# One indirect transfer for u and v rows, a ring of four groups of two, and dot products one group ahead

## The chip, the cores and the metric

The kernel runs on one core of a Trainium2 chip. The metric is the device time of one execution in microseconds (us). The core has TensorE (matrix products into PSUM), VectorE (DVE), ScalarE (ACT), GpSimd (POOL) and SyncE (SP), each with its own instruction queue, and 16 DMA engines between HBM and the on-chip SBUF. Engines meet only at semaphores.

## The reference

Two layers of a decoder trunk on 256 tokens of width 1024, all in float32. Each layer has a mixer (attention, pooling, a gated recurrence) and then a retrieval layer over 16384 single-neuron experts, which the change touches:

```
q = (xt @ w_query).reshape(T, 8, 2, 128)
s = einsum('thpd,pkd->thpk', q, sub_keys)
s_a, i_a = top_k(s[:, :, 0], 16);  s_b, i_b = top_k(s[:, :, 1], 16)
top_s, idx = top 16 of the 256 sums s_a + s_b   # expert = i_a * 128 + i_b
gate = softmax(top_s)
act = gelu(einsum('thkd,td->thk', u_tab[idx], x))
out = einsum('thk,thkd->td', gate * act, v_tab[idx])
```

For every token and each of 8 heads 16 experts are chosen; each brings a row of 1024 numbers of u and one of v. That is 256 x 8 x 16 x 2 rows of 4 KB per layer, 268 MB.

## The kernel before

The program is written by hand, with semaphores between engines. Per layer there is a mixer (a loop over pairs of its 8 heads) and then the expert stage. The expert stage is a loop over 8 heads. A head has 8 groups: 4 groups for the tokens 0 to 127 (`t` = 0) and 4 for the tokens 128 to 255 (`t` = 1); a group is 4 of the 16 chosen experts of each of the 128 tokens, one token to a partition. `gi` numbers the groups of a head from 0 to 7 and `q` those of a half from 0 to 3.

The order on each engine:

- GpSimd: `gather_u(gi + 1)` (L536), then `gather_v(gi)` (L546). Each issues four indirect transfers; one transfer brings one row of 4 KB to each of 128 partitions, 0.52 MB. u goes to `ubuf`, a ring of two groups of four rows in `wbuf[0]`; v to `vbuf`, the same in `wbuf[1]`. `gather_u` waits until the dot products two groups before are done, `gather_v` until the sum two groups before is done.
- VectorE: `dot_group(gi)` (recorded at L967, four reductions of 1024 elements, each with a small read of the accumulator), then a part of the routing for the next half, then `diag_group(gi)` (recorded at L961): four diagonal matrices of 128x128, with gate times gelu on the diagonal. The routing is `route_half` at `q` = 0 and 1 (top 16 of 128 scores, from L1284 on) and `route_pairs` with `route_end` at `q` = 2 (top 16 of the 256 sums, from the cast at L958 on, up to indices and gates).
- ScalarE: the gelu of each group (L681). At `gi` = 2 it then does the softmax exponentials of the routing (L675) and `q_evac(h + 1)`, the copy of the next head's queries from PSUM (L671). It does this before the gelu of group 3.
- TensorE: `expert_sum(gi)` (L922): for each of the four experts two matmuls of the diagonal with half a row of v, added up in PSUM, sixteen matmuls in all. After the sum of group 2 it makes the queries of the next head (`queries`, L900, 32 matmuls) and ahead of the sum of group 3 its key scores (`key_scores`, L910).
- SyncE loads the query weights of the next heads, 1 MB each, when the queries before them are done (L332). At the start of the second layer it loads the mixer's weights over `wbuf` (L349): the first part of `wbuf[0]` when the last dot products are done, that of `wbuf[1]` when the last sum is done.

After the last head VectorE adds the sums to the residual (`add_experts`, L1376 and L1378).

Of the kernel before, what the change touches and what calls it, by code (L numbers as in the profile page):

```python
# [25 lines left out]
P = 128  # L26
D = 1024
# [16 lines left out]
GROUP = 4  # L44
# [26 lines left out]
PEER_CHAIN = 99  # L71
# [9 lines left out]


def dotted(l):

    return (LGROUPS + 1) * l + 1
# [22 lines left out]
def build(nc, x, c, ada_w, ada_b, norm_mix_g, w_in, diff_lambda, diff_subln_g, pool_w, pool_scale,  # L108
          hgrn_lower_bounds, hgrn_norm_g, w_out, norm_ffn_g, peer_w_query, peer_sub_keys,
          peer_u, peer_v, final_g, out):  # L110
    with ExitStack() as ctx:
        def sb(name, shape, dt=F32):
            return ctx.enter_context(nc.sbuf_tensor(name, shape, dt))
# [21 lines left out]
        ubuf = wbuf[0][:, 0:2 * GROUP * D].rearrange("p (b s d) -> p b s d", b=2, s=GROUP)  # L135
        vbuf = wbuf[1][:, 0:2 * GROUP * D].rearrange("p (b s d) -> p b s d", b=2, s=GROUP)
# [25 lines left out]
        diag = M[:, 1024:2048].rearrange("p (b s n) -> p b s n", b=2, s=GROUP)  # L162
# [65 lines left out]
        dots = [sb(f"dots{b}", [P, GROUP]) for b in range(2)]  # L228
        gel = [sb(f"gel{b}", [P, GROUP]) for b in range(2)]
# [10 lines left out]
        s_u = [sem("s_u0"), sem("s_u1")]  # L240
        s_v = [sem("s_v0"), sem("s_v1")]
# [40 lines left out]
        u_rows = peer_u.rearrange("l e d -> (l e) d")  # L282
        v_rows = peer_v.rearrange("l e d -> (l e) d")


        WTAIL = range(-(-2 * GROUP * D // (SECT * P)), KC)
# [22 lines left out]
        def _(sp):  # L309
# [36 lines left out]
            for l in range(DEPTH):  # L346
# [22 lines left out]
                if l == 0:  # L369
                    load_w(0, 0)  # L370
                    sp.wait_ge(s_chunk, ADA_CHUNKS)
                    load_w(1, 1)
                else:

                    load_w(0, 0, WTAIL)
                    load_w(1, 1, WTAIL)
                    sp.wait_ge(s_dot, dotted(l - 1) + LGROUPS)
                    load_w(0, 0, range(WTAIL[0]))
                    sp.wait_ge(s_vacc, summed(l - 1) + LGROUPS)
                    load_w(1, 1, range(WTAIL[0]))  # L380
                    sp.wait_ge(s_peer, l)
                    load_bias_row(l, 2 * D, 6 * D)
# [39 lines left out]
        def _(pool):  # L422
# [49 lines left out]
            for l in range(DEPTH):  # L472
# [54 lines left out]
                def gather_u(h, gi):  # L527
                    t, q = gi // GROUPS, gi % GROUPS
                    if q == 0:
                        pool.wait_ge(s_route, h * NT + (2 * HEADS * l + t + 1))  # L530
                    if l or gi or not isinstance(h, int) or h:
                        pool.wait_ge(s_dot, h * HGROUPS + (dotted(l) + gi - 1))
                    apart(pool)
                    for s in range(GROUP):
                        k = q * GROUP + s
                        nc.gpsimd.indirect_dma_start(  # L536
                            out=ubuf[:, gi % 2, s, :], out_offset=None, in_=u_rows,
                            in_offset=bass.IndirectOffsetOnAxis(ap=idx[t][:, k:k + 1], axis=0)).then_inc(s_u[gi % 2], 16)

                def gather_v(h, gi):  # L540
                    t, q = gi // GROUPS, gi % GROUPS
                    pool.wait_ge(s_vacc, h * HGROUPS + (summed(l) + gi - 1))
                    apart(pool)
                    for s in range(GROUP):
                        k = q * GROUP + s
                        nc.gpsimd.indirect_dma_start(  # L546
                            out=vbuf[:, gi % 2, s, :], out_offset=None, in_=v_rows,
                            in_offset=bass.IndirectOffsetOnAxis(ap=idx[t][:, k:k + 1], axis=0)).then_inc(s_v[gi % 2], 16)

                def head(h, more):  # L550
                    for gi in range(HGROUPS):
                        if gi + 1 < HGROUPS:
                            gather_u(h, gi + 1)
                        elif more:
                            gather_u(h + 1, 0)
                        gather_v(h, gi)

                gather_u(0, 0)
                with pool.Fori(0, HEADS - 1) as h:
                    head(h, True)  # L560
                head(HEADS - 1, False)
# [4 lines left out]
        def _(act):  # L566
# [11 lines left out]
            for l in range(DEPTH):  # L578
# [110 lines left out]
                route_exp(0, 0)  # L689
                with act.Fori(0, HEADS - 1) as h:  # L690
                    head(h, True)
# [4 lines left out]
        def _(pe):  # L696
# [26 lines left out]
            for l in range(DEPTH):  # L723
# [171 lines left out]
                def queries(h):  # L895

                    pe.wait_ge(s_r[0], h * 16 + 16 * (ADA_CHUNKS // 4 + (HEADS - 1) * l))
                    for a in range(2):
                        for k in range(KC):
                            i = mm(bank(B_Q)[:, a * T:(a + 1) * T], ringv[0][:, k, a * P:(a + 1) * P], hT[:, k, :],  # L900
                                   start=(k == 0), stop=(k == KC - 1))
                    i.then_inc(s_chunk, 1)
# [11 lines left out]
                def expert_sum(h, gi, last=False):  # L914

                    t = gi // GROUPS
                    pe.wait_ge(s_diag, h * HGROUPS + (LGROUPS * l + gi + 1))
                    pe.wait_ge(s_v[gi % 2], h * (16 * HGROUPS * GROUP // 2)
                               + 64 * (LGROUPS // 2 * l + gi // 2 + 1))
                    for s in range(GROUP):  # L920
                        for hf in range(2):
                            i = mm(bank(B_ACC + 2 * t + hf), diag[:, gi % 2, s, :],  # L922
                                   vbuf[:, gi % 2, s, hf * 512:(hf + 1) * 512], start=False,
                                   stop=(last and s == GROUP - 1), skip_group_check=True)
# [12 lines left out]
                for b in range(4):  # L937
                    i = mm(bank(B_ACC + b), diag[:, 1, GROUP - 1, :], hT[:, 0:2, :], start=True, stop=False,
                           skip_group_check=True)
                    i.then_inc(s_vacc, 1)  # L940
# [12 lines left out]
        def _(dve):  # L953
# [118 lines left out]
            for l in range(DEPTH):  # L1072
# [205 lines left out]
                v.memset(dots[1][:], 0.0).then_inc(s_dot, 1)  # L1278
                v.memset(diag[:, 1, GROUP - 1, :], 0.0).then_inc(s_cb, 1)
# [68 lines left out]
                def dot_group(h, gi):  # L1348
                    t = gi // GROUPS
                    dve.wait_ge(s_u[gi % 2], h * (16 * HGROUPS * GROUP // 2) + 64 * (LGROUPS // 2 * l + gi // 2 + 1))  # L1350

                    for s in range(GROUP):
                        u = ubuf[:, gi % 2, s, :]
                        i = dot(u, u, tok[:, t, :], dots[gi % 2][:, s:s + 1])
                        if s < GROUP - 1:
                            ch(i)
                    i.then_inc(s_dot, 1)

                def diag_group(h, gi):
                    t, q = gi // GROUPS, gi % GROUPS  # L1360
                    dve.wait_ge(s_gel, h * HGROUPS + (LGROUPS * l + gi + 1))
                    dve.wait_ge(s_vacc, h * HGROUPS + (summed(l) + gi - 1))
                    for s in range(GROUP):
                        k = q * GROUP + s
                        i = sts(diag[:, gi % 2, s, :], ident[:], gel[gi % 2][:, s:s + 1], gate[t][:, k:k + 1],
                                ALU.mult, ALU.mult)
                        if s < GROUP - 1:
                            ch(i)
                    i.then_inc(s_diag, 1)
# [10 lines left out]
                def head(h, more):  # L1380
                    for gi in range(HGROUPS):
                        if gi == HGROUPS - 2 and not more:
# [3 lines left out]
                        dot_group(h, gi)  # L1386
# [11 lines left out]
                        ch.sync()  # L1398
# [5 lines left out]
                route_end(0, 0, True)  # L1404
                start = ch.n
# [20 lines left out]
        "peer_u", "peer_v", "final_g"]  # L1426
# [16 lines left out]
```

## Time and profile before

| | |
|---|---|
| time, median of 3 runs | 2810.35 us (2802.63 to 2813.17) |
| span of the profiled execution | 2765.2 us; its own time is not given apart, so the median of the runs stands beside it |
| expert stage, core 0 | about 604 to 1410 us and 1950 to 2750 us |
| busy over the span | PE 76%, DVE 69%, POOL 57%, ACT 12% |
| DMA | 715 MB, of which 536.94 MB in the indirect gathers; mean 259 GB/s |
| indirect gathers | 1024, half of them u and half v |

The span is the time from the first to the last instruction of the core in the execution that the profiler recorded; what the metric counts beyond it lies before and after. Times in the profile are counted from the start of the span. An engine's line in the profile carries the line number of the code that recorded it, its operation, what it wrote and what it read. "Idle before" is how long the engine stood before that instruction, and the arrow names what ended the standing.

### The profile page before, as it was taken

The numbers are of one execution on the slowest core, as the hardware profiler recorded it, in microseconds if no ns is written. First come the engines' busy times: TensorE is split into PE (matmuls) and PEld (weight loads), VectorE is DVE, ScalarE is ACT, GpSimd is POOL, SyncE is SP. The second block draws the span as 40 slices with busy tenths as digits, with TensorE's granted clock in tenths as the row PEclk, the third lists the DMA queues.
The fourth block names the chain that finished last, engine by engine and source line by source line (L and its number), as shares of the span: only waits on it lengthen the run. The fifth ranks groups of instructions, "written<-read, shape, count | busy, mean of one in ns | idle before, by whom it ended". The sixth has DMA issues, their size and how long they took to land.

```text
span 2765.2 us, 23903 instructions
## 1 busy us (share of the span) xinstructions
PE 2103.5 (76%) x6485; PEld 1236.6 (45%) x6485; DVE 1907.0 (69%) x4313; ACT 333.0 (12%) x696; POOL 1582.3 (57%) x1421
## 2 busy tenths in 40 slices
PE   6988887757777777867779889896577767767766
PEld 5766665533333323323247657664233323323322
DVE  3588888956666576675635888888566576576664
ACT  0211112100011011010002221120011011011010
POOL 1445554436766776776731433332667776676775
PEclk9989898778898989988889988997799998989988
DMA  9645555239999999998973565421799999999996
GB/s 310 172 130 142 137 151 164 77 134 329 364 340 359 365 342 347 361 381 322 359 227 104 146 169 147 114 98 63 269 341 359 371 329 335 357 346 340 335 357 252
DMA packets 405255, 715.06 MB, mean 259 GB/s; under 512 B 20667, under 2 KB 270803, under 8 KB 405075
## 3 DMA queue, kind: packets, MB, share of 16 engines
q0 software_dynamic: 147456, 536.94, 52.6%
q1 hardware_dynamic: 257750, 177.54, 22.6%
q8 instruction: 22, 0.36, 0.1%
q14 instruction: 27, 0.22, 0.0%
HBM read 713.35 MB, written 1.05 MB: 258 GB/s over the span
## 4 chain that ended last, share of the span: by engine, by line
PE 29%; POOL 22%; DVE 21%; issue 17%; DMA 8%; ACT 2%; SPq 1%; DVEq 0%; POOLq 0%; ACTq 0%
POOL wbuf L536 12%; PE PS L922 10%; POOL wbuf L546 9%; DMA wbuf<-in_peer_v,idx 7%; PE PS L749 5%; PE PS L900 4%; PE PS L812 3%; PE PS L744 3%; DVE M L1101 3%; DVE wbuf L967 2%; DVE ring L964 2%; DVE ring L1173 2%; DVE ring L1172 1%; DVE tok L964 1%; ACT ring L632 1%
## 5 line engine op out<-in xcount | busy, mean ns | idle before, releaser
L922 PE MATMUL PS<-wbuf,M 128*128 128x512 f32 x2048 | 1040.7, 667 | 451.5 <-DMA wbuf<-in_peer_v,idx 421.6
L922 PEld LDWEIGHTS PS<-wbuf,M 128*128 128x128 f32 x2048 | 427.1, 214 | 1054.8 <-issue 845.0
L536 POOL DMA_INDIRECT wbuf<-in_peer_u,idx x512 | 652.8, 1275 | 301.9 <-issue 152.0
L967 DVE CUSTOM_DVE_ANT_0 wbuf<-wbuf,tok 128x1024 f32<-128x1024 f32 x512 | 597.6, 1222 | 256.9 <-DMA wbuf<-in_peer_u,idx 256.6
L546 POOL DMA_INDIRECT wbuf<-in_peer_v,idx x512 | 498.7, 974 | 160.5 <-issue 154.6
L961 DVE TENSOR_SCALAR M<-ident,gel,gate 128x128 f32<-128x128 f32 x512 | 144.0, 355 | 266.9 <-ACT gel L681 248.5
L744 PE MATMUL PS<-hT,wbuf 128*128 128x256 f32 x1280 | 285.1, 382 | 6.0 <-DMA wbuf<-in_w_in 5.2
L467 POOL TENSOR_SCALAR rsb<-ms 128x4 f32<-128x4 f32 (+2 forms) x23 | 4.4, 193 | 481.3 <-DVE ms L967 481.3
L744 PEld LDWEIGHTS PS<-hT,wbuf 128*128 128x128 f32 x1280 | 243.6, 191 | 41.3 <-issue 6.7
L749 PE MATMUL PS<-wbuf,hT 128*128 128x512 f32 x512 | 231.3, 606 | 0.0
L485 POOL TENSOR_TENSOR braw<-braw,cact 128x1024 f32<-128x1024 f32 x80 | 154.2, 1928 | 65.8 <-DMA braw<-in_ada_w 65.8
L812 PE MATMUL PS<-ring 128*128 128x64 f32 x448 | 93.3, 401 | 128.2 <-DVE ring L1195 128.2
L812 PEld LDWEIGHTS PS<-ring 128*128 128x128 f32 x448 | 90.8, 313 | 140.8 <-DVE ring L1195 139.8
L681 ACT ACTIVATE gel<-dots 128x4 f32<-128x4 f32 x128 | 26.3, 205 | 1049.3 <-DVE dots L967 1049.1
L749 PEld LDWEIGHTS PS<-wbuf,hT 128*128 128x128 f32 x512 | 99.8, 198 | 112.9 <-issue 112.1
L754 PE MATMUL PS<-wbuf,hT 128*128 128x256 f32 x512 | 113.1, 379 | 0.0
L487 POOL TENSOR_TENSOR braw<-braw 128x512 f32<-128x512 f32 x80 | 107.9, 1349 | 6.3
L1118 DVE RECIPROCAL M<-M 128x1024 f32<-128x1024 f32 x16 | 104.8, 6553 | 0.6
L754 PEld LDWEIGHTS PS<-wbuf,hT 128*128 128x128 f32 x512 | 96.7, 190 | 13.7 <-issue 1.0
L900 PE MATMUL PS<-hT,ring 128*128 128x256 f32 x448 | 99.0, 379 | 0.0
L900 PEld LDWEIGHTS PS<-hT,ring 128*128 128x128 f32 x448 | 85.1, 190 | 17.5 <-issue 6.7
L1101 DVE RECIPROCAL M<-M 128x768 f32<-128x768 f32 x16 | 79.2, 4953 | 0.6
(223 smaller groups left out, 2130.4 us busy)
## 6 DMA issues: line engine op xcount, KB each, us to landing
wbuf<-in_w_in SPq DMA_DIRECT2D x128, 704.0 KB, 8.6
braw<-in_ada_w SPq DMA_DIRECT2D x80, 512.0 KB, 3.7
ring<-in_peer_w_query SPq DMA_DIRECT2D x16, 1024.0 KB, 8.5
wbuf<-in_w_out SPq DMA_DIRECT2D x2, 4096.0 KB, 16.0
wbuf<-in_peer_u,idx POOLq DMA_INDIRECT x512, 6.1
wbuf<-in_peer_v,idx POOLq DMA_INDIRECT x512, 6.2
ring<-in_ada_w SPq DMA_DIRECT2D x4, 1024.0 KB, 9.2
wbuf<-in_ada_w SPq DMA_DIRECT2D x4, 1024.0 KB, 12.0
```

The costliest lines, as they stand in the source:

```text
L485: pc(tt(w, w, cact[:, 4 * s:4 * s + 4].unsqueeze(2).to_broadcast([P, 4, CH]), ALU.mult))
L536: nc.gpsimd.indirect_dma_start(out=ubuf[:, gi % 2, s, :], out_offset=None, in_=u_rows, in_offset=bass.IndirectOffsetOnAxis(ap=idx[t][:, k: ...
L546: nc.gpsimd.indirect_dma_start(out=vbuf[:, gi % 2, s, :], out_offset=None, in_=v_rows, in_offset=bass.IndirectOffsetOnAxis(ap=idx[t][:, k: ...
L744: ins = mm(b[:, i * T:(i + 1) * T], wz[j][:, k, s, :], hT[:, k, :], start=(k == 0), stop=(k == KC - 1))
L749: ins = mm(b, hT[:, k, t * P:(t + 1) * P], wz[j][:, k, HI:ZP + 1, :], start=(k == 0), stop=(k == KC - 1))
L754: ins = mm(b[:, t * 256:(t + 1) * 256], hT[:, k, t * P:(t + 1) * P], wz[j][:, k, AV:ZR + 1:ZR - AV, :], start=(k == 0), stop=(k == KC - 1))
L812: mm(bank(b)[:, o + 64 * ck:o + 64 * ck + 64], XD[:, lv, ck * P:(ck + 1) * P], right, start=True, stop=True)
L900: i = mm(bank(B_Q)[:, a * T:(a + 1) * T], ringv[0][:, k, a * P:(a + 1) * P], hT[:, k, :], start=(k == 0), stop=(k == KC - 1))
L922: i = mm(bank(B_ACC + 2 * t + hf), diag[:, gi % 2, s, :], vbuf[:, gi % 2, s, hf * 512:(hf + 1) * 512], start=False, stop=(last and s == GR ...
L961: return v.tensor_scalar(o, a, s1, s2, op0, op1)
L967: return v.tensor_tensor_reduce(out=o, in0=a, in1=b, scale=1.0, scalar=0.0, op0=ALU.mult, op1=ALU.add, accum_out=acc)
L1101: ch(v.reciprocal(e, e))
```

## The change

The u and v tables come to the kernel as one table `peer_uv`, in which the 1024 numbers of u and the 1024 of v of an expert lie side by side. One indirect transfer brings both, 8 KB to each of 128 partitions. A group is now 2 experts instead of 4, so a head has 16 groups, 8 for each half. The ring has four slots, two in each `wbuf`, each of two experts with u and v; they take the same space as before. A slot is gathered again when the sum of the group in it is done.

VectorE does the dot products of group `gi + 1` ahead of the routing part and the diagonals of group `gi`; ScalarE does the gelu likewise one group ahead. The routing parts still stand at `q` = 0, 1 and 2. On TensorE the queries are split in two, after the sums of groups 2 and 3, and the key scores come after the sum of group 5. On ScalarE the copy of the queries stands at `gi` = 5, after the gelu of group 6.

```
-GROUP = 4
+GROUP = 2
+NBUF = 4
...
+        PAIRED = 2 * GROUP * 2 * D
+        uvbuf = [wbuf[b // 2][:, (b % 2) * (PAIRED // 2):(b % 2 + 1) * (PAIRED // 2)].rearrange("p (s d) -> p s d", s=GROUP)
+                 for b in range(NBUF)]
...
-                    sp.wait_ge(s_dot, dotted(l - 1) + LGROUPS)
+                    sp.wait_ge(s_vacc, summed(l - 1) + LGROUPS - 2)
                     load_w(0, 0, range(WTAIL[0]))
...
+                def gather(h, gi):
                     t, q = gi // GROUPS, gi % GROUPS
+                    b = gi % NBUF
                     if q == 0:
                         pool.wait_ge(s_route, h * NT + (2 * HEADS * l + t + 1))
-                    if l or gi or not isinstance(h, int) or h:
-                        pool.wait_ge(s_dot, h * HGROUPS + (dotted(l) + gi - 1))
+                    if gi >= NBUF or not isinstance(h, int) or h:
+                        pool.wait_ge(s_vacc, h * HGROUPS + (summed(l) + gi - NBUF + 1))
                     apart(pool)
                     for s in range(GROUP):
                         k = q * GROUP + s
                         nc.gpsimd.indirect_dma_start(
+                            out=uvbuf[b][:, s, :], out_offset=None, in_=uv_rows,
+                            in_offset=bass.IndirectOffsetOnAxis(ap=idx[t][:, k:k + 1], axis=0)).then_inc(s_uv[b], 16)
...
+                def gelu(h, gi):
+                    act.wait_ge(s_dot, h * HGROUPS + (LGROUPS * l + gi + 1))
+                    nc.scalar.activation(gel[gi % NBUF][:], dots[gi % NBUF][:], ACT.Gelu).then_inc(s_gel, 1)
+
                 def head(h, more):
                     for gi in range(HGROUPS):
-                        act.wait_ge(s_dot, h * HGROUPS + (dotted(l) + gi + 1))
-                        nc.scalar.activation(gel[gi % 2][:], dots[gi % 2][:], ACT.Gelu).then_inc(s_gel, 1)
+                        if gi + 1 < HGROUPS:
+                            gelu(h, gi + 1)
+                        elif more:
+                            gelu(h + 1, 0)
                         if gi == 2:
                             route_exp(h, 1)
-                            if more:
-                                q_evac(h + 1)
+                        if gi == 5 and more:
+                            q_evac(h + 1)
                         if gi == GROUPS + 2 and more:
                             route_exp(h + 1, 0)
...
                 def head(h, more):
                     for gi in range(HGROUPS):
-                        if more and gi == 3:
+                        expert_sum(h, gi, not more and gi % GROUPS == GROUPS - 1)
+                        if more and gi in (2, 3):
+                            queries(h + 1, gi - 2)
+                        if more and gi == 5:
                             key_scores(h + 1)
-                        expert_sum(h, gi, not more and gi % GROUPS == GROUPS - 1)
-                        if more and gi == 2:
-                            queries(h + 1)
...
-                        dot_group(h, gi)
+                        if gi + 1 < HGROUPS:
+                            dot_group(h, gi + 1)
+                        elif more:
+                            dot_group(h + 1, 0)
                         t, q = gi // GROUPS, gi % GROUPS
...
                             elif q == 2:
                                 route_pairs(nh, nt)
                                 route_end(nh, nt, False)
-                        ch.sync()
+                                ch.sync()
                         diag_group(h, gi)
```

## Rows read from the trace of the kernel before

**Rows 1.** The page's costliest groups: count, busy us and mean ns, idle before.

```profile
L922 PE MATMUL PS<-wbuf,M 128*128 128x512 f32 x2048 | 1040.7, 667 | 451.5 <-DMA wbuf<-in_peer_v,idx 421.6
...
L536 POOL DMA_INDIRECT wbuf<-in_peer_u,idx x512 | 652.8, 1275 | 301.9 <-issue 152.0
...
L546 POOL DMA_INDIRECT wbuf<-in_peer_v,idx x512 | 498.7, 974 | 160.5 <-issue 154.6
```

**Rows 2.** The waits of GpSimd: us in total, times, longest.

```profile
POOL wbuf L546 <- issue: 154.6, 507, 0.3
POOL wbuf L536 <- issue: 152.0, 472, 6.7
POOL wbuf L536 <- DVE dots L967: 104.6, 13, 10.2
```

**Rows 3.** The chain that ended last, queries of two heads: start us, us, what.

```profile
659.59 6.92 PE PS L900 x32
...
1253.22 6.92 PE PS L900 x32
```

**Rows 4.** The timeline around the queries of one head: start us, us, instruction, idle before.

```profile
765.93 0.60 ACT L671 ACTIVATE M<-PS 128x512 f32<-128x512 f32 x1 [24.53 <-PE PS L900]
...
767.84 0.21 ACT L681 ACTIVATE gel<-dots 128x4 f32<-128x4 f32 x1
...
768.24 1.11 DVE L961 TENSOR_SCALAR M<-ident,gel,gate 128x128 f32<-128x128 f32 x4 [18.12 <-ACT gel L681]
769.27 1.22 DVE L967 CUSTOM_DVE_ANT_0 wbuf<-wbuf,tok 128x1024 f32<-128x1024 f32 x1
...
773.86 0.08 DVE L967 DVE_READ_ACCUMULATOR2_ANT dots<- 128x1 f32 x1
...
774.71 0.94 POOL L536 DMA_INDIRECT wbuf<-in_peer_u,idx  x1 [8.77 <-DVE dots L967]
```

**Rows 5.** Stretches of 4 us; last three columns: PE clock, DMA share, GB/s.

```profile
652.00:656.00 4.00, 4.00 (x7) 1.55 (x6) 0.00 (x0) 0.00 (x0) 3.08 (x4) 0.59 0.94 338
...
660.00:664.00 4.00, 4.00 (x21) 3.51 (x20) 0.00 (x0) 0.00 (x0) 2.91 (x4) 1.00 1.03 422
664.00:668.00 4.00, 3.31 (x19) 2.68 (x18) 0.00 (x0) 1.45 (x2) 0.94 (x1) 1.00 1.03 412
...
672.00:676.00 4.00, 4.00 (x10) 1.73 (x10) 3.69 (x13) 0.21 (x1) 0.70 (x1) 1.00 0.16 52
```

**Rows 6.** Line L536, first and fourth gather of the stage, each with its landing.

```profile
L536 POOL DMA_INDIRECT wbuf<-in_peer_u,idx x1: 1222/1222/1222, 603.6 to 603.6; - x1
...
DMA to landing us min/median/max: 4.4/4.4/4.4
...
L536 POOL DMA_INDIRECT wbuf<-in_peer_u,idx x1: 937/937/937, 607.6 to 607.6; - x1
...
DMA to landing us min/median/max: 6.0/6.0/6.0
```

**Rows 7.** The timeline of VectorE: start of a routing half, of the pairs, and diagonals behind.

```profile
618.24 0.29 DVE L1284 MAX8 sv<-PS 128x8 f32<-128x128 f32 x1
...
620.35 1.12 DVE L961 TENSOR_SCALAR M<-ident,gel,gate 128x128 f32<-128x128 f32 x4 [0.23 <-DVE iu L1287]
...
636.67 0.18 DVE L958 CAST idf<-iu 128x32 f32<-128x32 uint32 x1
...
643.53 1.11 DVE L961 TENSOR_SCALAR M<-ident,gel,gate 128x128 f32<-128x128 f32 x4
```

**Rows 8.** The timeline of TensorE: sums of a group after short and long idleness.

```profile
637.25 7.11 PE L922 MATMUL PS<-wbuf,M 128*128 128x512 f32 x16 [1.85 <-DMA wbuf<-in_peer_v,idx]
...
649.68 9.90 PE L922 MATMUL PS<-wbuf,M 128*128 128x512 f32 x16 [5.33 <-DMA wbuf<-in_peer_v,idx]
...
792.03 8.69 PE L922 MATMUL PS<-wbuf,M 128*128 128x512 f32 x16 [7.77 <-DMA wbuf<-in_peer_v,idx]
```

**Rows 9.** The chain that ended last, the last sum of the first layer.

```profile
1401.66 8.82 PE PS L922 x16
```

More of the change, by code:

```diff
@@ L109, in build @@
           hgrn_lower_bounds, hgrn_norm_g, w_out, norm_ffn_g, peer_w_query, peer_sub_keys,
-          peer_u, peer_v, final_g, out):
+          peer_uv, final_g, out):
     with ExitStack() as ctx:
@@ L227, in build @@
         gate = [sb(f"gate{t}", [P, TOPK]) for t in range(2)]
-        dots = [sb(f"dots{b}", [P, GROUP]) for b in range(2)]
-        gel = [sb(f"gel{b}", [P, GROUP]) for b in range(2)]
+        dots = [sb(f"dots{b}", [P, GROUP]) for b in range(NBUF)]
+        gel = [sb(f"gel{b}", [P, GROUP]) for b in range(NBUF)]
         s_par, s_x, s_bias, s_gain = sem("s_par"), sem("s_x"), sem("s_bias"), sem("s_gain")
@@ L239, in build @@
         s_pused = sem("s_pused")
-        s_u = [sem("s_u0"), sem("s_u1")]
-        s_v = [sem("s_v0"), sem("s_v1")]
+        s_uv = [sem(f"s_uv{b}") for b in range(NBUF)]
         s_out = sem("s_out")
@@ L281, in build @@
         wq_v = [peer_w_query[l].rearrange("(k p) n -> p k n", p=P) for l in range(DEPTH)]
-        u_rows = peer_u.rearrange("l e d -> (l e) d")
-        v_rows = peer_v.rearrange("l e d -> (l e) d")
-        WTAIL = range(-(-2 * GROUP * D // (SECT * P)), KC)
+        uv_rows = peer_uv.rearrange("l e d -> (l e) d")
+        WTAIL = range(-(-PAIRED // (SECT * P)), KC)
         def brow(v, n):
@@ L536, in gather_u, with head @@
                         nc.gpsimd.indirect_dma_start(
[L537 to L550, printed above, removed]
-                    for gi in range(HGROUPS):
[L552 to L561, printed above, removed]
+                            out=uvbuf[b][:, s, :], out_offset=None, in_=uv_rows,
+                            in_offset=bass.IndirectOffsetOnAxis(ap=idx[t][:, k:k + 1], axis=0)).then_inc(s_uv[b], 16)
+                def head(h):
+                    for gi in range(HGROUPS):
+                        gather(h, gi)
+                head(0)
+                with pool.Fori(1, HEADS) as h:
+                    head(h)
             rsqrt(NR * DEPTH, NT, D)
@@ L689, in _ @@
                 route_exp(0, 0)
+                gelu(0, 0)
                 with act.Fori(0, HEADS - 1) as h:
@@ L893, in _, with queries @@
                         i.then_inc(s_psc0, 1)
[L895 to L902, printed above, removed]
+                def queries(h, a):
+                    if a == 0:
+                        pe.wait_ge(s_r[0], h * 16 + 16 * (ADA_CHUNKS // 4 + (HEADS - 1) * l))
+                    for k in range(KC):
+                        i = mm(bank(B_Q)[:, a * T:(a + 1) * T], ringv[0][:, k, a * P:(a + 1) * P], hT[:, k, :],
+                               start=(k == 0), stop=(k == KC - 1))
+                    if a == 1:
+                        i.then_inc(s_chunk, 1)
                 def key_scores(h):
@@ L917, in expert_sum @@
                     pe.wait_ge(s_diag, h * HGROUPS + (LGROUPS * l + gi + 1))
[L918 to L919 removed]
                     for s in range(GROUP):
                         for hf in range(2):
[L922 to L923 removed]
+                            i = mm(bank(B_ACC + 2 * t + hf), diag[:, gi % NBUF, s, :],
+                                   uvbuf[gi % NBUF][:, s, D + hf * 512:D + (hf + 1) * 512], start=False,
                                    stop=(last and s == GROUP - 1), skip_group_check=True)
@@ L1277, in _ @@
                 dve.wait_ge(s_tok, 3 * l + 3)
-                v.memset(dots[1][:], 0.0).then_inc(s_dot, 1)
-                v.memset(diag[:, 1, GROUP - 1, :], 0.0).then_inc(s_cb, 1)
+                v.memset(diag[:, NBUF - 1, GROUP - 1, :], 0.0).then_inc(s_cb, 1)
                 def top8(vals, ids, src):
@@ L1348, in dot_group @@
                 def dot_group(h, gi):
-                    t = gi // GROUPS
-                    dve.wait_ge(s_u[gi % 2], h * (16 * HGROUPS * GROUP // 2) + 64 * (LGROUPS // 2 * l + gi // 2 + 1))
+                    t, b = gi // GROUPS, gi % NBUF
+                    per = HGROUPS // NBUF * 16 * GROUP
+                    dve.wait_ge(s_uv[b], h * per + (per * HEADS * l + 16 * GROUP * (gi // NBUF + 1)))
                     for s in range(GROUP):
-                        u = ubuf[:, gi % 2, s, :]
-                        i = dot(u, u, tok[:, t, :], dots[gi % 2][:, s:s + 1])
+                        u = uvbuf[b][:, s, 0:D]
+                        i = dot(u, u, tok[:, t, :], dots[b][:, s:s + 1])
                         if s < GROUP - 1:
@@ L1381, in head @@
                     for gi in range(HGROUPS):
-                        if gi == HGROUPS - 2 and not more:
+                        if gi == HGROUPS - 4 and not more:
                             ch(add_experts(0))
@@ L1404, in _ @@
                 route_end(0, 0, True)
+                ch.sync()
+                dot_group(0, 0)
                 start = ch.n
```

20 lines of the change are left out of this document (8 added, 12 removed).

## The prediction

> **What bounds the kernel now.** I read the page's costliest groups first, to see that the expert stage (TensorE L922, GpSimd L536 and L546, VectorE L967) is where the time is [rows 1]; then the waits of GpSimd; then the chain of waits for the length of a head; then the timeline of one head. The stage runs from the first gather at 603.6 us to the end of the last sum at 1401.66 + 8.82 = 1410.5 us [rows 6, 9]: 806.9 us per layer, of which a head takes (1253.22 - 659.59) / 6 = 98.9 us [rows 3]. Two layers of it are 58% of the span.
>
> In this stage GpSimd does nothing but issue gathers. Over both layers it is busy 652.8 + 498.7 us, has 152.0 + 154.6 us of issue gaps of 0.3 us, and waits 104.6 us for dot products [rows 1, 2]: 1562.7 us of two stages of 806.9. So the issuing queue is the pace. A gather costs it (652.8 + 498.7 + 306.6) / 1024 = 1.42 us on average, eight per group of four pairs of rows, 11.4 us; that is 91 us of a head's 98.9. The transfers are just behind: 412 to 422 GB/s where GpSimd issues without a break, 52 GB/s where it stopped [rows 5]. A head's 32 pairs of 1.049 MB and its 1.05 MB of query weights are 34.6 MB, at 412 GB/s 84 us.
>
> The 104.6 us have one cause, which comes once per head. ScalarE stands 24.53 us in the copy of the query scores (L671), because TensorE makes the queries only after group 2's sum; the gelu of group 3 is queued behind it, VectorE stands 18.12 us before the diagonals of group 3, the dot products of group 4 come late, and GpSimd stands 8.77 us [rows 4].
>
> **What the change takes away.** (a) Half of the 1024 issues. If a row of 8 KB costs an issue what one of 4 KB does, GpSimd has 32 x 1.42 = 45 us of work in a head where it had 91: the present bound is gone. If it costs as for two rows, 1.88 us busy instead of 0.94, GpSimd still has room (32 x 2.2 = 70 us). (b) The copy of the queries stands behind the gelu of group 6, two groups after the last query matmul, so ScalarE's stall, and 104.6 us of GpSimd's waiting, go. Both together would leave the transfers as the bound.
>
> **What it adds: a longer loop through the ring.** Before, a u slot was free at its dot products and a v slot was asked for later than its u. Now one slot holds both until the sum. With four slots, the chain is: diagonals of group i, sum of i, slot free, gather of i+4, dot products of i+4, diagonals of i+3 (VectorE does them in that order). That is three groups per turn. Its terms, for groups of two:
> - diagonals 0.6 (four take 1.11 to 1.13, rows 4 and 7);
> - sum 3.7: sixteen matmuls take 7.11 warm [rows 8], eight half of that and the end of the pipeline;
> - slot free to issue 0.75: dot end 773.86 + 0.08 to issue 774.71 [rows 4];
> - landing of the pair of transfers, 2.1 MB, from the start of the first issue: not shown by this trace. The same bytes as four u transfers took 607.6 + 6.0 - 603.6 = 10.0 us [rows 6]. That is the upper end for equal work, as the new second issue comes at 1.24 us and not at 4.0. The lower end: the first 0.52 MB took 4.4 us, 3.15 beyond its 1.25 at 421 GB/s, and 2.1 MB at that rate are 5.0, so 8.1 us. I take 8.9, near the middle. A transfer path quicker with long rows could go below, at the very least to the 4.4 us of a quarter of the bytes; I carry 7 as a point between, near the upper of the two.
> - two dot products 2.3: four run from 769.27 to 773.94 [rows 4].
>
> Sum 16.25 us for three groups, 5.4 us per group, where the transfers alone would ask 5.0. A head of 16 groups would be 87 us were there nothing else. The loop has thus no slack, and whatever stands between a dot product and its diagonals, or before a sum, comes on top:
> - routing on VectorE, twice a head: a half 620.35 - 618.24 = 2.1 (two of them), the pairs 643.53 - 636.67 = 6.8 [rows 7]. Before they lay under 11.4 us of issuing per group; now they stand in a group of 5.4.
> - queries on TensorE after sums 2 and 3: 6.92 in all, 3.5 each [rows 3]; key scores, eight matmuls of half that width, after sum 5: under 8/32 of 6.92 = 1.7, taken as 1.3.
> - TensorE's clock: with 1.85 us of idleness before them sixteen matmuls take 7.11, with 5.33 they take 9.90, with 7.77 8.69 [rows 8]. After the 5.33 the granted clock was 0.59 over 652 to 656 us, so mostly the 1.2 GHz level, and 1.00 from 660 [rows 5]. A sum that starts on the low level costs 1.6 to 2.8 more, say 2.3; I call it cold.
>
> I walked through a head with these terms: dot products of i+1 at the later of their landing and VectorE's being free; then routing; then diagonals of i; sum at the later of that and TensorE's being free; landing of i+4 9.65 after the sum, and at least 5.0 after the landing before it (7.5 once, with the query weights). Diagonals start, with a warm TensorE, at 0, 5.0, 14.7 (pairs), 17.6, 21.2, 30.9, 38.1, 45.4, 52.5, 60.0, 69.6 (pairs), 72.5, 76.2, 85.9, 90.9, 95.9, and the next head's first at 104.3. One sees it at group 5: sum 2 ends at 19.0, its slot's next pair lands at 28.6, and so diagonals 5 start at 30.9, although VectorE could have been there at 24. The 6.8 us of the pairs are never won back, since group 5 waits for the slot of group 2. TensorE idles 4.6, 6.0, 6.0 and 5.1 us before sums 0, 2, 10 and 13; all four cold give 111.1 per head, two of them about 107.7. I take 107.7: 6.0 lies above the 5.33 that was cold, the others near it.
>
> **Sum.** Per layer: first diagonals 18.3 us after the first gather (8.9, 5.0 for the second group, 2.3, half a routing 2.1); seven heads of 107.7, 754; the last head, without second routing and queries but with 4 us of adding the first half's result, 90 us to the end of its last sum. Together 862 for 806.9, so +55; both layers +110. The span 2765.2 would be 2875; outside the span lie 2810.35 - 2765.2 = 45 us (taken from the median, since the profiled execution's own time is not given apart), which stay. 2810 + 110 = 2920; the four-cold walk gives 895 per layer and +177, and with a share of that I say 2925.
>
> Edits costed at nothing: the reload of the next layer's weights waits for the sum of group 13 instead of the last dot product. It lies under the last sums; if that cover is gone it costs at most one sum of 8.8 us [rows 9], once. Semaphores and the missing memset are single instructions. 64 more gelus per layer at 0.21 us [rows 4] go to ScalarE, busy for 12% of the span. The smaller groups at the start and end save a few us per layer and are in the walk.
>
> The Trainium skill ("DMA: Bandwidth & Descriptors", section "Anatomy of one DMA — SWDGE (gpsimd) path") gives a transfer 2.0 us fixed and bytes over 436 GB/s, which speaks for fewer, larger gathers. By that a 0.52 MB gather would be 3.2 us, where the row shows 4.4 from the start of the issue; a pair would be 6.8 us by it, plus the issue. No run here shows a gather of 8 KB rows.
>
> **The rivals.**
> 1. The ring keeps up and the transfers are the bound, the change doing all it could: 34.6 MB at 412 GB/s, 84 us a head, about 690 a layer, -234 in all: 2575. For it: 422 GB/s in rows 5 and GpSimd's bound gone. Against: the walks with landings of 7.95 and 7 (rival 2) give 101.4 and 99.2 per head, and on that slope 84 would need a landing under 1 us. The chance of 0.04 is for an error in the walk.
> 2. The pair lands quicker and TensorE stays warm. The walk with 8.1 (near it 7.95) gives 101.4 per head and 811 per layer, +8 in all; with 7, 99.2 and 793, -28: 2782. It decides from a landing of 7.7 us downward. For it: fewer issues and descriptors. Against: nothing in rows 6 lands 2.1 MB under 8.1. The 6.8 us worked out above from the Trainium skill's page would fall to this rival. Chance 0.13 of being faster by it, 0.06 of no change.
> 3. Issuing 8 KB rows costs double, 0.94 us more on each of the two issues. The landing becomes 10.8; the walk with 10 gives 924 per layer (four cold) and about 3 us per head and us more: +280, 3090. For it: unknown descriptors. Against: an issue may go by rows, of which there are still 128. Chance 0.1.
> 4. The change doesn't do what it says: ScalarE's stall comes back in another place, as the gelu of group 7 is behind the copy. The queries are then two groups old; 3.5 us of stall per head at most, +50 on the forecast: 2975. Chance 0.07.
> 5. The forecast, 2925, its own range 2840 to 3000: chance 0.6.
>
> Slower by over 0.5% (14 us, about what a measurement of this kernel can tell from no change): 0.6 + 0.1 + 0.07 = 0.77; faster 0.04 + 0.13 = 0.17; same 0.06. For 8 in 10 the range goes from 2800, which takes in the walk with 8 us, to 3010; the 2 in 10 outside are rivals 1, 3 and half of 2.
>
> **What would show it.** Right: GpSimd's waits in the stage for TensorE's sum (L922), several us per group, in place of its issue gaps and of the 104.6; the transfers below 350 GB/s with dips after groups 2 and 10; a head of 104 to 111 us; DVE waiting for the gather, most before group 5's or 13's. ScalarE's copy of the queries without a wait of 20 us. Wrong: landings of a pair under 7.5 us, a head under 98, or rates steady above 390 GB/s. Then the loop is shorter than I walked it and the forecast falls.

## The result, and the profile after

The changed kernel takes 3003.8 us (2997.1 to 3005.3 in 4 runs), the kernel before 2806.5 in the runs beside it: a ratio of 1.070, interval 1.068 to 1.073. Slower by 197 us; the forecast was slower, by 115, and the time lies just inside the upper end of the range, 3010.

The costliest groups of the page (count, busy us and mean ns, idle before), to be read beside [rows 1]:

```profile
L909 PE MATMUL PS<-wbuf,M 128*128 128x512 f32 x2048 | 1112.2, 700 | 636.6 <-DVE M L948 635.9
L954 DVE CUSTOM_DVE_ANT_0 wbuf<-wbuf,tok 128x1024 f32<-128x1024 f32 x512 | 607.4, 1223 | 767.4 <-DMA wbuf<-in_peer_uv,idx 767.4
...
L532 POOL DMA_INDIRECT wbuf<-in_peer_uv,idx x512 | 547.0, 1068 | 1294.4 <-PE PS L909 1108.5
```

GpSimd's 1024 issues of 1151.5 us together are now 512 of 547.0. The mean of one is 1068 ns, where u had 1275 and v 974 (the medians are 937, 940 and 938): a row of 8 KB costs the issue what one of 4 KB did. The 104.6 us behind ScalarE's copy [rows 2] are gone. In their place stand 1108.5 us of waiting for the sum. The issuing queue has been freed, and it now waits for a slot ten times as long as it waited for dot products before.

The transfers show what that is worth. The middle of the first stage, in the kernel before and then in the changed one, and three stretches of one head of the changed kernel (last columns: TensorE clock, DMA share, GB/s):

```profile
700.00:1300.00 600.00, 443.85 (x1016) 204.44 (x1015) 388.45 (x1030) 56.94 (x109) 433.35 (x390) 0.89 0.96 353
...
700.00:1300.00 600.00, 399.69 (x878) 182.03 (x877) 331.74 (x873) 49.19 (x129) 181.19 (x168) 0.83 0.78 304
812.00:816.00 4.00, 4.00 (x9) 1.69 (x8) 4.00 (x9) 0.27 (x2) 0.00 (x0) 0.75 0.00 0
816.00:820.00 4.00, 4.00 (x11) 1.85 (x10) 0.41 (x2) 0.13 (x1) 1.87 (x2) 1.00 0.37 88
824.00:828.00 4.00, 0.00 (x0) 0.00 (x0) 1.96 (x3) 0.00 (x0) 1.63 (x2) 0.96 1.01 414
```

304 GB/s on average, where the kernel before moved 353 in the same window. It is not that 8 KB rows are slow: they run at 414 as soon as slots are free. At 812 to 816 nothing moves at all: the pairs of groups 10 to 13 have landed in the four slots, and the sum of group 10, which frees the first of them, is still running.

One turn of the ring, in the timeline of all engines (start us, us, instruction, idle before; rows not belonging to this slot left out):

```profile
752.26 0.60 DVE L948 TENSOR_SCALAR M<-ident,gel,gate 128x128 f32<-128x128 f32 x2 [0.20 <-DVE gate L948]
...
752.92 5.21 PE L909 MATMUL PS<-wbuf,M 128*128 128x512 f32 x8 [5.92 <-DVE M L948]
...
758.90 0.94 POOL L532 DMA_INDIRECT wbuf<-in_peer_uv,idx  x1 [8.95 <-PE PS L909]
...
766.87 1.23 DVE L954 CUSTOM_DVE_ANT_0 wbuf<-wbuf,tok 128x1024 f32<-128x1024 f32 x1 [5.04 <-DMA wbuf<-in_peer_uv,idx]
...
769.17 0.60 DVE L948 TENSOR_SCALAR M<-ident,gel,gate 128x128 f32<-128x128 f32 x2
```

The diagonals of group 2 start at 752.26, its sum at 752.92; 0.77 us after the sum the slot is gathered again; the new pair has landed 7.97 later; two dot products, and at 769.17 come the diagonals of group 5. Every step waits for the one above it: 16.9 us for three groups, 5.6 each. And the head as a whole, by the queries after group 2's sum in two successive heads:

```profile
757.96 3.62 PE L888 MATMUL PS<-hT,ring 128*128 128x256 f32 x16
...
870.71 3.62 PE L888 MATMUL PS<-hT,ring 128*128 128x256 f32 x16
```

112.75 us. It is the shortest of the six such distances in the first stage: they go up to 118.1, and their mean is 115.0, where the mean before was 98.9 [rows 3]. The 98.9 comes from a quick execution of the kernel before (see the account of the prediction), so these 16 us overstate a little what the change costs a head.

### The profile page after: what moved, and what is told of

The parts are those of the page before. It is cut to its first block, busy times and chain, and to the rows that moved or that the text cites. A ratio compares the mean times of both kernels' runs of the same rounds, so it can differ in the third digit from the quotient of the medians.

```text
span 3000.9 us, 23732 instructions
## 1 busy us (share of the span) xinstructions
PE 2165.8 (72%) x6485; PEld 1257.8 (42%) x6485; DVE 1910.0 (64%) x4311; ACT 341.8 (11%) x812; POOL 977.3 (33%) x909
## 3 DMA queue, kind: packets, MB, share of 16 engines
HBM read 713.35 MB, written 1.05 MB: 238 GB/s over the span
## 4 chain that ended last, share of the span: by engine, by line
PE 37%; DVE 25%; DMA 21%; issue 13%; POOL 2%; ACT 1%; SPq 1%; DVEq 1%; POOLq 0%
DMA wbuf<-in_peer_uv,idx 20%; PE PS L909 19%; PE PS L737 5%; PE PS L888 3%; PE PS L800 3%; PE PS L732 2%; DVE M L1088 2%; DVE ring L951 2%; DVE wbuf L954 2%; DVE ring L1160 2%; DVE M L948 1%; POOL wbuf L532 1%; DVE ring L1159 1%; DVE tok L951 1%; DVE ts L1270 1%
## 5 line engine op out<-in xcount | busy, mean ns | idle before, releaser
L909 PE MATMUL PS<-wbuf,M 128*128 128x512 f32 x2048 | 1112.2, 700 | 636.6 <-DVE M L948 635.9
L954 DVE CUSTOM_DVE_ANT_0 wbuf<-wbuf,tok 128x1024 f32<-128x1024 f32 x512 | 607.4, 1223 | 767.4 <-DMA wbuf<-in_peer_uv,idx 767.4
L909 PEld LDWEIGHTS PS<-wbuf,M 128*128 128x128 f32 x2048 | 447.9, 226 | 1273.1 <-DVE M L948 765.1
L532 POOL DMA_INDIRECT wbuf<-in_peer_uv,idx x512 | 547.0, 1068 | 1294.4 <-PE PS L909 1108.5
L661 ACT ACTIVATE gel<-dots 128x2 f32<-128x2 f32 x256 | 52.2, 204 | 1630.5 <-DVE dots L954 1630.5
L948 DVE TENSOR_SCALAR M<-ident,gel,gate 128x128 f32<-128x128 f32 x512 | 152.6, 341 | 5.2 <-DVE gate L948 4.3
L742 PEld LDWEIGHTS PS<-wbuf,hT 128*128 128x128 f32 x512 | 96.7, 190 | 13.7 <-issue 1.0
L1160 DVE TENSOR_TENSOR ring<-bs 128x128 f32<-128x128 f32 x112 | 66.3, 592 | 0.0
```

Source lines behind the costliest of these rows:

```text
L532: nc.gpsimd.indirect_dma_start(out=uvbuf[b][:, s, :], out_offset=None, in_=uv_rows, in_offset=bass.IndirectOffsetOnAxis(ap=idx[t][:, k:k + ...
L742: ins = mm(b[:, t * 256:(t + 1) * 256], hT[:, k, t * P:(t + 1) * P], wz[j][:, k, AV:ZR + 1:ZR - AV, :], start=(k == 0), stop=(k == KC - 1))
L909: i = mm(bank(B_ACC + 2 * t + hf), diag[:, gi % NBUF, s, :], uvbuf[gi % NBUF][:, s, D + hf * 512:D + (hf + 1) * 512], start=False, stop=(l ...
L948: return v.tensor_scalar(o, a, s1, s2, op0, op1)
L954: return v.tensor_tensor_reduce(out=o, in0=a, in1=b, scale=1.0, scalar=0.0, op0=ALU.mult, op1=ALU.add, accum_out=acc)
L1160: ch(v.tensor_tensor(dv[:, :, 0, :], mid, bv[:, :, 0, :], ALU.subtract))
```

## The experiments

Theory: the time is set by a turn of the ring, which brings only three groups because dot products run one group ahead. Rivals: the 8 KB transfer itself; the order on VectorE as such; the written-out loops; TensorE's clock; and, for the kernel before, that its 104.6 us were transfers' time in disguise.

| run | ratio to before, interval | a head, mean of six, us |
|---|---|---|
| the change | 1.070, 1.068 to 1.073 | 115.0 |
| e1, before, copy later | 0.973, 0.970 to 0.977 | 97.9 |
| e2, dots not ahead | 0.963, 0.958 to 0.967 | 97.3 |
| e3, split rows | 1.093, 1.089 to 1.096 | 120.1 |
| e4, ring of five | 0.961, 0.957 to 0.964 | 96.7 |
| e5, written out, ring of four | 1.068, 1.066 to 1.071 | 113.8 |
| e6, TensorE kept busy | 1.076, 1.073 to 1.079 | 116.4 |
| e7, ring of five, dots not ahead | 0.911, 0.908 to 0.913 | 88.7 |
| e8, groups of one, ring of eight | 0.930, 0.928 to 0.932 | 91.8 |
| e9, TensorE kept busy less | 1.058, 1.053 to 1.063 | 109.5 |
| e10, groups of one, ring of ten | 0.915, 0.911 to 0.918 | 84.8 |
| e11, the same, dots not ahead | 0.914, 0.911 to 0.918 | 84.8 |

A head is the distance of two heads' queries in the timeline of the first stage, and the table has the mean of the six. The runs of e9 to e11 were on a chip on which the kernel before takes 2755 us, those of e1 to e4 on one with 2816, those of e5 to e8 on one with 2808; so ratios are compared, and not microseconds. The heads come from single profiled executions and carry the difference between the chips.

**e1, one part of the change alone, on the kernel before.**

```diff
                         if gi == 2:
                             route_exp(h, 1)
-                            if more:
-                                q_evac(h + 1)
+                        if gi == 3 and more:
+                            q_evac(h + 1)
```

> The kernel before, with one part of the change: ScalarE copies the next head's queries behind the gelu of group 3 instead of ahead of it. Theory (GpSimd's issuing is the bound of the kernel before, and its only pauses, 104.6 us in all, come from this copy): the pauses go and the time falls by 80 to 105 us, ratio to before 0.963 to 0.971. Rival (the transfers take the place of the pause: 34.6 MB per head are 84 us at 412 GB/s, but at the mean rate of the stage, 348 GB/s, 99): the pauses go and the issues stretch; under 30 us gained, ratio 0.99 to 1.0.

2740.2 us, for 2816.1: 76 us gained, just short of the lower end of the theory's 80. The pause for dot products is gone, and part of it is given back as new waits (us in total, times, longest):

```profile
DVE sv L1284 <- remote: 100.4, 8, 14.9
...
POOL wbuf L546 <- PE PS L922: 71.3, 12, 14.7
...
DVE sv L1284 <- PE PS L910: 46.0, 4, 17.8
```

VectorE, no longer late, reaches the routing of the next head (L1284) before the key scores (L910) are there; the profile can't name the releaser of eight of these twelve waits, but the instruction is the same. So what was a wait for the gelu is in part a wait for the scores. The 71.3 us that GpSimd waits for the sum are new too; that they follow from this wait is argued, not isolated. The mean rate in the window is 355 GB/s, for 353 before; but that 353 is of an execution of about 2767 us, and not of the 2816 that e1 is set against, so the two rates do not measure the gain. This part of the change was good by itself: 2.7%. The other parts took 9.7 points.

**e2, dot products back in their own turn.**

```diff
-                        if gi + 1 < HGROUPS:
-                            dot_group(h, gi + 1)
-                        elif more:
-                            dot_group(h + 1, 0)
+                        dot_group(h, gi)
...
-                        if gi + 1 < HGROUPS:
-                            gelu(h, gi + 1)
-                        elif more:
-                            gelu(h + 1, 0)
+                        gelu(h, gi)
```

> The changed kernel with dot products and gelu of a group back in its own turn, the ring of four and the 8 KB rows kept. Theory (the time is set by the turn of the ring: slot free, gather, landing, dot products, diagonals, sum, and one group ahead makes a turn bring three groups instead of four): a turn of 16 to 17 us brings four groups, 4.2 us each, so the transfers (5.0) and the clumps of routing remain; a head 95 to 100 us instead of 112.8, time 2740 to 2810, ratio to before 0.975 to 1.0. Rival (8 KB transfers land late, the order on VectorE doesn't matter or helps by hiding the gelu): time 3000 or more, ratio 1.07 or above.

2706.1 us, a head of 97.3: the theory, and a little better than its 2740 and its ratio of 0.975. With the other parts of the change kept, the order alone turns 7% slower into 3.7% faster. The price of the gelu that the order was meant to hide, and the wait that it caused, in this run:

```profile
POOL wbuf L532 <- PE PS L905: 832.4, 220, 12.0
...
DVE wbuf L950 <- DMA wbuf<-in_peer_uv,idx: 420.2, 168, 10.6
...
DVE M L944 <- ACT gel L661: 50.2, 164, 0.4
```

50.2 us of waiting for the gelu bring VectorE's wait for the gather from 767.4 down to 420.2.

**e3, the rows split again, all else as changed.** The four issues per group are u and v of each expert in turn, to the same slot:

```diff
-                        nc.gpsimd.indirect_dma_start(
-                            out=uvbuf[b][:, s, :], out_offset=None, in_=uv_rows,
+                        for part_, rows in ((uvbuf[b][:, s, 0:D], u_rows), (uvbuf[b][:, s, D:2 * D], v_rows)):
+                            nc.gpsimd.indirect_dma_start(
+                                out=part_, out_offset=None, in_=rows,
```

> The changed kernel with u and v rows of 4 KB from two tables by two indirect transfers again, into the same slots, all else as changed. Theory (the ring's turn): the turn becomes longer, since the last of four issues comes 2.5 us later and a pair lands in 10 instead of 9 us, and each issue costs GpSimd as before; a head 113 to 119 us, ratio to before 1.07 to 1.11. Rival (the 8 KB transfer itself is what costs): the time falls back towards before, ratio under 1.04.

3076.9 us, ratio 1.093, a head of 120.1 (the theory's 113 to 119, passed a little). So the paired transfer is not what cost; even in this ring it is worth 2 points.

**e4, a fifth slot; e5, its control.** `pair(n, s)` gives the place of expert `s` of group `n`, counted through all heads; the first four slots are those of the changed kernel. The cut shows the main lines; the two comments are added here.

```diff
+        spare = (M[:, 4352:4352 + 2 * D], ring[1][:])
+        def pair(n, s):
+            slot = n % DEEP                      # 5 in e4, 4 in e5
+            return uvbuf[slot][:, s, :] if slot < 4 else spare[s]
...
-                    if gi >= NBUF or not isinstance(h, int) or h:
-                        pool.wait_ge(s_vacc, h * HGROUPS + (summed(l) + gi - NBUF + 1))
+                    if gi >= DEEP or h:
+                        pool.wait_ge(s_vacc, h * HGROUPS + (summed(l) + gi - DEEP + 1))
...
-                with dve.Fori(0, HEADS - 1) as h:      # and so on every engine
+                for h in range(HEADS):
```

> The changed kernel with a fifth slot of two experts (in free space beside the routing buffers and in the second query buffer), the loops over the heads written out so that the slot number can run through; dot products still one group ahead. Theory (the ring's turn): a turn brings four groups instead of three, as in the run with dot products in their own turn; a head 95 to 100 us, ratio to before 0.975 to 1.01. Rival (transfers, TensorE's clock or VectorE's clumps are the bound and not the number of slots): a head of 108 to 113, ratio 1.05 to 1.07.

> The changed kernel with the loops over the heads written out and the ring still of four slots: what the run with five slots has beside its fifth slot. Theory (the number of slots in the turn made that run's gain): no gain here, ratio to before 1.06 to 1.075. Rival (the written-out loops and the waits on constants made it): ratio 0.96 to 1.0.

e4 takes 2705.7 us (0.961), better than the 0.975 to 1.01 expected and the same as e2 within its interval; e5 takes 2997.0 (1.068), the same as the change. One slot more and one group less ahead are worth the same 11 points of the ratio, some 300 us: in both, a turn brings four groups. Loops and constants are worth nothing.

**e7, both.** It is e4 with e2's edit.

> Both remedies: five slots, and dot products in their own turn. Theory (the turn of the ring was the bound and each remedy gave it one group more; with five groups in a turn of some 17 us it is shorter than the five transfers, 25 us, and only the clump of the pairs and the transfers remain): a head 87 to 92 us, time 2590 to 2670, ratio to before 0.92 to 0.95. Rival (either remedy alone already reached another bound, VectorE's order or the transfers): within 15 us of the 2706 of each alone, ratio 0.955 to 0.97.

2557.6 us beside 2807.7, ratio 0.911, better than the 0.92 to 0.95 expected, and the best ratio of all. The same window as above:

```profile
700.00:1300.00 600.00, 473.40 (x1118) 219.92 (x1119) 442.62 (x1149) 64.09 (x169) 229.37 (x218) 0.91 0.99 398
```

The DMA share is 0.99 at 398 GB/s: in this stretch the transfers bind, and there is nearly nothing left for a longer ring to gain.

**e8, e10, e11, smaller groups.** `GROUP = 1` and `NBUF = 8`; routing parts at `q` = 0, 2, 4, queries behind the sums of groups 5 and 7, key scores behind 11. e10 and e11 add two slots in the same spare places.

> The ring's space as in the changed kernel, cut into eight slots of one expert instead of four of two, dot products one slot ahead, loops written out; routing, queries and key scores at the same points of a head. Theory (a slot is held while its group is filled, waited for and summed; groups of one make that shorter in the same space): a turn of about 11 us brings seven experts, 3.1 us for two; a head 86 to 93 us, ratio to before 0.92 to 0.95. Rival (twice the semaphore steps on VectorE, ScalarE and TensorE cost what the shorter turn gives): ratio 0.98 to 1.05.

> Groups of one expert, ten slots in the space of the ring of five, dot products one slot ahead. If the transfers are the last bound, at 398 GB/s over the middle of the first stage in the run with five slots and dot products not ahead, this comes to within 20 us of its 2558 (ratio 0.905 to 0.92). If what is left in that run is VectorE's wait for the gelu, 94.8 us, which this order hides, it falls below 2530.

> The same with dot products in their own turn: the gelu is waited for twice as often (about 0.45 us for each of 512 groups of one, 230 us of VectorE in all), beside a shorter hold of each slot. If the transfers are the bound, within 20 us of 2558 like the other; if VectorE's serial work per expert (1.2 dot, 0.45 wait, 0.3 diagonal, and 21 us of routing per head: 84 us a head) has become it, 30 to 80 us slower.

e8: 2612.1 us, 0.930, a head of 91.8, in exactly the ring's space of the changed kernel and with the dot products ahead: the finer grain alone takes 13% off the changed kernel's time (the loops written out are worth nothing, e5). e10 and e11 both move 403 GB/s at shares of 0.99 and 1.00 in the window, and their ratios, 0.915 and 0.914, can't be told apart, nor e10's from e7's 0.911 with certainty (intervals touch, chips differ). e11 waits 157.9 us for the gelu and e10 13.9, without a difference in time. Of the two ways that e11 was expected to go, the loss from VectorE's serial work did not come, and the transfers as last bound did. The microseconds that these two expectations gave stand for the chip of e7 and can't be compared; 2517 and 2515 here are beside a kernel before of 2755.

**e6 and e9, TensorE's clock.** Matmuls whose result nobody reads, behind five sums of each head:

```diff
+                        for _ in range({1: 9, 6: 5, 9: 16, 12: 8, 15: 13}.get(gi, 0)):
+                            mm(bank(3)[:, 0:T], ident[:], hT[:, 0, :], start=True, stop=True)
```

(e9; in e6 16, 10, 32, 16 and 24.)

> The changed kernel with TensorE kept busy in its idle stretches by matmuls whose result nobody reads: 16, 10, 32, 16 and 24 of 256 columns behind the sums of groups 1, 6, 9, 12 and 15 of each head. Theory (sums that start at the low clock lengthen the turn of the ring by 1.4 to 3 us, five times a head, and not all of it is hidden): the granted clock rises above 0.92 in the stage, a sum that follows such a stretch takes 3.7 instead of 5 to 6.5 us, a head loses 4 to 7 us, ratio to before 1.03 to 1.05. Rival (the clock costs nothing, the landings set the pace, or the added matmuls delay the sums as much): ratio 1.065 to 1.08.

> As the run before with TensorE kept busy, with half the added work, since each such matmul took 0.44 us and not the 0.22 reckoned with, so that the sums behind waited for it: now 9, 5, 16, 8 and 13 of them behind the sums of groups 1, 6, 9, 12 and 15, 2.2 to 7.1 us into gaps of 4.5 to 9.6. Theory (starts at the low clock lengthen the ring's turn): clock above 0.92, no sum waits for the added work, a head 4 to 7 us shorter than 112.8, ratio to before 1.03 to 1.05. Rival (landings set the pace whatever the clock): ratio 1.06 to 1.075.

e6 gave the rival's number, 1.076, but for a reason in its own design (timelines of TensorE and VectorE; L950 are the diagonals that the sum needs):

```profile
800.17 13.98 PE L918 MATMUL PS<-hT,ident 128*128 128x256 f32 x64
...
807.83 0.60 DVE L950 TENSOR_SCALAR M<-ident,gel,gate 128x128 f32<-128x128 f32 x2 [0.20 <-DVE gate L950]
...
813.99 10.46 PE L909 MATMUL PS<-wbuf,M 128*128 128x512 f32 x24
```

The added work takes 14 us where the gap was 9.6. The sum starts 6.2 us after the start of its diagonals, where a sum that finds TensorE free starts 0.65 after it (752.26 and 752.92 above): it waited 5.5 us for the added work.

In e9 the clock over the whole execution is 0.922 instead of 0.845 and the ratio 1.058 [1.053 to 1.063]; a head of 109.5. That is neither the 1.03 to 1.05 of the theory nor, by its middle, the 1.06 to 1.075 of the rival. Here the sum in the same place doesn't wait for the added work, as it starts 0.65 after its diagonals:

```profile
791.69 7.07 PE L918 MATMUL PS<-hT,ident 128*128 128x256 f32 x32
...
797.99 0.60 DVE L950 TENSOR_SCALAR M<-ident,gel,gate 128x128 f32<-128x128 f32 x2 [0.20 <-DVE gate L950]
798.64 3.70 PE L909 MATMUL PS<-wbuf,M 128*128 128x512 f32 x8
```

The traces show that the low clock stands in the chain. In the six heads behind the first, of both stages, the sums of groups 2 and 10 take 6.2 and 6.3 us in the changed kernel and 4.4 and 4.1 in e9, and the turns from the diagonals of group 2 to those of 5, and of 10 to 13, take 19.3 and 19.0 us in the one and 17.3 and 17.0 in the other: each turn is shorter by about what its sum is. How much of the time that makes is less sure. By the ratios it is 1.2 points, some 35 us, between 0.5 and 2.0 points by the two intervals; and that takes it that the change's 1.070 holds on the chip of e9, where the changed kernel was not run. The microseconds differ by 93, of which the kernel before gains 51 between the same two chips.

## Why the prediction was right

**What the change takes away: right; the bound before: in part argued.** The issue of a transfer of 8 KB rows costs 0.94 us, as in [rows 4], so GpSimd's load halved (rival 3 is out), and ScalarE's copy no longer waits for the queries or holds a gelu (it starts at 769.40 without idle time; rival 4 is out). e1 gives the second part its own number, 76 us. That the issuing queue alone was the pace is not isolated: the DMA share of the kernel before was 0.96 in the window shown above, so its transfers were nearly as close a bound as the prediction said, or closer.

**The longer loop: right, term by term.** 0.6 for the diagonals, 3.7 for a warm sum, 0.77 from slot to issue (0.75), 2.3 for the dot products. The landing, which no row of before showed, was taken as 8.9 from bounds of 8.1 and 10.0. In one head of after, counted to the dot products that wait for it, it is 7.97 (758.90 to 766.87), 8.94 (765.79 to 774.73), 8.91 (792.02 to 800.93), 9.16 (816.88 to 826.04) and 9.55 (836.18 to 845.73); 10.2 (772.68 to 782.89) where the query weights had been asked for before it, and 11.8 where the pair before was still under way. The first of the stage took 9.3. None of these lies under the 7.7 from which rival 2 decides. The Trainium skill's fit ("DMA: Bandwidth & Descriptors", section "Anatomy of one DMA — SWDGE (gpsimd) path") gave a pair 6.8 us by the prediction's estimate; this trace does not agree, with 7.97 at the least of those read.

**The walk.** The first diagonals come 18.3 us after the first gather (603.29 to 621.55), as summed. In the head from 736.82 the diagonals start at 0, 5.0, 15.4, 19.4, 24.4, 32.4, 40.2, 48.4, 55.2, 60.1, 73.4, 76.2, 79.0, 91.5, 96.5, 101.4, and the next head's at 113.0. To group 9 that is within 3.2 us of the walk with a warm TensorE; the pairs' 6.8 us at groups 2 and 10 are never won back, as it said. VectorE's longest waits for a gather come before the diagonals of groups 5 and 13, also as it said. Its sign of a head of 104 to 111 us was missed: the six distances of the first stage are 112.8 to 118.1.

**What was too small.** In the sum, a stage was to take 862 us; the two take 921 (603.3 to 1524.7) and 927. The term that was mis-sized is the number of sums that start on the low clock: two a head (107.7), with four as the other walk (111.1). It is five. Three of them, by the timeline of TensorE:

```profile
752.92 5.21 PE L909 MATMUL PS<-wbuf,M 128*128 128x512 f32 x8 [5.92 <-DVE M L948]
...
785.84 5.40 PE L909 MATMUL PS<-wbuf,M 128*128 128x512 f32 x8 [4.46 <-DVE M L948]
...
810.85 12.12 PE L909 MATMUL PS<-wbuf,M 128*128 128x512 f32 x24 [9.61 <-DVE M L948]
```

The other two start after 6.02 us of idleness at 828.99 and after 7.91 at 850.47. In the six heads behind the first, of both stages, the sums of groups 0, 2, 7, 10 and 13 take 5.7, 6.2, 5.9, 6.3 and 5.7 us, where a warm one takes 3.6 to 3.7; so the 2.3 us for one were right, and group 7, which the walk had warm, was among them. The walk by its own rules with these five comes to 112.2 a head, an estimate, for the 115.0 measured; the remaining 2.8 us a head are not isolated. The landings of 10 to 12 us of pairs that queue are no mis-sized term: the walk, with its 5.0 and 7.5 us between landings, has them as well. The last head, costed at 90 us, took 100 from its first diagonals to the end of its last sum; that part is not explained here. That the low clock has a share is shown by e9; how the difference between forecast and measured divides is argued from these rows.

**A step that was wrong, and helped.** I put 45 us outside the span, as the difference of the median and the span of the profile. The changed kernel's profiled execution took 3002.6 us with a span of 3000.9: 1.7 lie outside. The profiled execution of before was therefore itself one of about 2767 us, faster than the runs in the table; chips differ by that much (medians of the same kernel of 2755, 2808 and 2816 us in three places). The quicker chip is also the one that shows the higher granted clock: 0.880 to 0.886 in the seven runs with the median of 2755, 0.863 to 0.873 in the fourteen others, and 0.883 in the profile of before. Between the two profiled executions the change costs 236 us, where the sum had 110 for the stages; a difference of the two spans overstates the change by the difference of the executions, and 197 is what like runs show. But without the 45 us the forecast would have been 2880, and the range as much lower would have ended at 2965. That the time fell inside the range is thus in part luck.

**Rival 1**, the transfers as the bound at 84 us a head, was possible after all, only not with this ring: e7 comes to 88.7.

## What to carry to other kernels

When buffers are merged, count the hold: a slot that serves two consumers is held from its gather to the later of them, and running the first consumer ahead adds a whole group to that. With few slots, divide the turn (free, issue, landing, use) by the slots left after the run-ahead, and compare with the transfer time of one. Here 16.3 / 3 against 5.0 said before the change was built that the loop had no slack. By itself it gave 87 us a head; the rest of the 115 are the routing, the queries and the sums on the low clock, which a loop without slack can't hide. More and smaller slots in the same space, or one step less ahead, repair it; here a freed issue queue gained nothing, as it then waited for a slot.

## What the hardware showed that was not expected

An indirect transfer of 128 rows costs GpSimd the same 0.94 us whether rows are 4 or 8 KB (median 940 ns before, 937 after), but up to 1.98 us when a dot product has begun on VectorE shortly before: the issue at 760.14 us of the changed kernel, 0.05 us behind the start of one, takes 1.97. Of the 91 issues over 1.2 us in that trace 90 start during a dot product. The landing of one 1.05 MB transfer, in the half of the 512 for which the profile gives it, varied from 5.4 to 15.1 us, median 8.5; the longer ones of the head read above had other transfers ahead of them. The gathers and the query weights reached 403 GB/s as a mean over 600 us (e10, e11); single 4 us stretches show up to 426 (the changed kernel, 780 to 788 us).
